# A two-block transformer forward pass in split precision: operand placement, attention bias tables, running sums, and GpSimd's part of the weight splits

## The reference

```
# first block
h = rmsnorm(x, norm_mix)
proj = h @ w_in           # z, xbc, dt | b q,k,v | c q,k,v, f | d q,kv | 4 gates of 1024
y_a = mamba2(...)         # causal conv, silu, y = (cb * exp(cum_l - cum_s)) @ (x dt), rmsnorm (ssm_norm_w)
y_b = softmax(q k / 8 + bias(distance), causal) @ v                 # "MoBA", one block of 256 here
y_c = softmax(q k / 8 + cum_f[q] - cum_f[k], causal) @ v            # "forgetting attention"
y_d = softmax(q k / 8 + bias(distance), window 128, with sinks) @ v # sliding window, 2 kv heads
x = x + (sum_i sigmoid(gate_i) * (y_i @ w_branch_i)) @ w_out
x = x + (silu(h2 @ w_gate) * (h2 @ w_up)) @ w_down                  # h2 = rmsnorm(x), inner width 2816
x = rmsnorm(x, norm_final)
# second block: two layers
x = x + hgrn2(rmsnorm(x)) ; x = x + swiglu(rmsnorm(x))
x = x + rglru(rmsnorm(x)) ; x = x + swiglu(rmsnorm(x)) ; out = rmsnorm(x)
```

## Time and profile before

| | us |
|---|---|
| three runs | 1255.49, 1258.89, 1253.69 (median 1255.49) |
| profiled execution | 1250.67 |
| its span | 1249.4 |

### The profile page before, as it was taken

How to read it: one execution, slowest core, us unless ns; L and a number is a source line. 1 busy time by engine, 2 the same in 40 slices (tenths; PEclk the granted TensorE clock), 3 DMA queues, 4 the chain that set the end, 5 groups by cost and what they waited for, 6 DMA issues and landing times.

```text
span 1249.4 us, 19584 instructions
## 1 busy us (share of the span) xinstructions
PE 1194.6 (96%) x8237; PEld 1096.5 (88%) x8237; DVE 682.3 (55%) x965; ACT 591.9 (47%) x901; POOL 473.1 (38%) x253
## 2 busy tenths in 40 slices
PE   7979999999989999999899999999999769999998
PEld 6979898788878999988898879999889768999986
DVE  5742644366756645334789757433326696633423
ACT  6534544445444554444652345444334674544432
POOL 4345333233231444441654423444423350543440
PEclk9989999999989999999999999999999879999999
DMA  7585465344445666564543435755555333756560
GB/s 240 163 265 154 145 197 144 108 121 125 128 135 152 184 188 187 187 200 143 182 134 135 151 120 171 217 177 185 196 185 173 114 135 118 217 181 187 177 199 34
DMA packets 160833, 204.75 MB, mean 164 GB/s; under 512 B 13535, under 2 KB 135577, under 8 KB 160746
## 3 DMA queue, kind: packets, MB, share of 16 engines
q1 hardware_dynamic: 154650, 193.69, 49.9%
q0 software_dynamic: 1840, 6.64, 1.6%
q10 hardware_dynamic: 4256, 3.16, 0.8%
HBM read 202.38 MB, written 1.09 MB: 163 GB/s over the span
## 4 chain that ended last, share of the span: by engine, by line
PE 78%; DVE 12%; ACT 6%; issue 2%; SPq 1%; ACTq 1%; DMA 0%; POOL 0%; DVEq 0%
PE bank L488 15%; PE bank L491 15%; PE bank L494 15%; PE bank L505 9%; PE bank L511 9%; PE bank L508 9%; ACT whi L947 2%; DVE wlo L1360 2%; DVE sm L1649 1%; PE bank L846 1%; DVE Ss L1780 1%; DVE ring L1651 1%; DVE uc L1490 1%; DVE qT L1774 1%; DVE ring L1637 1%
## 5 line engine op out<-in xcount | busy, mean ns | idle before, releaser
L1920 POOL TENSOR_TENSOR wlo<-raw,whi 128x1024 fp32r<-128x1024 f32 (+1 forms) x161 | 411.6, 2559 | 545.4 <-ACT whi L947 545.4
L947 ACT ACTIVATE whi<-raw 128x1024 fp32r<-128x1024 f32 x368 | 364.9, 1041 | 125.7 <-PE bank L511 117.0
L1360 DVE TENSOR_TENSOR wlo<-raw,whi 128x1024 fp32r<-128x1024 f32 x207 | 277.9, 1352 | 258.9 <-ACT whi L947 257.9
L488 PE MATMUL bank<-hh,whi 128*128 128x256 f32 x1792 | 293.7, 286 | 1.7 <-ACT hh L979 1.7
L491 PE MATMUL bank<-hh,wlo 128*128 128x256 f32 x1792 | 289.4, 284 | 0.9 <-DVE wlo L1360 0.9
L494 PE MATMUL bank<-hl,whi 128*128 128x256 f32 x1792 | 289.0, 284 | 0.0
L488 PEld LDWEIGHTS bank<-hh,whi 128*128 128x128 f32 x1792 | 248.8, 193 | 11.1 <-issue 9.9
L491 PEld LDWEIGHTS bank<-hh,wlo 128*128 128x128 f32 x1792 | 248.3, 193 | 1.4 <-DVE wlo L1360 1.4
L494 PEld LDWEIGHTS bank<-hl,whi 128*128 128x128 f32 x1792 | 248.4, 193 | 0.0
L505 PE MATMUL bank<-whi,gh 128*128 128x512 f32 x264 | 83.4, 397 | 0.0
L511 PE MATMUL bank<-whi,gl 128*128 128x512 f32 x264 | 83.1, 395 | 0.0
(11 more groups left out here) (296 smaller groups left out, 1319.0 us busy)
## 6 DMA issues: line engine op xcount, KB each, us to landing
raw<-in_ffn_w_in SPq DMA_DIRECT2D x88, 512.0 KB, 3.6
raw<-in_w_in SPq DMA_DIRECT2D x72, 512.0 KB, 3.7
raw<-in_ffn_w_out SPq DMA_DIRECT2D x44, 512.0 KB, 3.2
raw<-in_hgrn_w_in SPq DMA_DIRECT2D x32, 512.0 KB, 4.0
raw<-in_w_ffn_gate SPq DMA_DIRECT2D x22, 512.0 KB, 4.6
raw<-in_w_ffn_up SPq DMA_DIRECT2D x22, 512.0 KB, 4.1
raw<-in_w_ffn_down SPq DMA_DIRECT2D x22, 512.0 KB, 3.3
raw<-in_w_branch SPq DMA_DIRECT2D x16, 512.0 KB, 4.1
```

The lines of the kernel that those rows point to most:

```text
L488: T.matmul(out, wh[:, i, c], xh[:, k, :], start=first and (i, k) == pairs[0], stop=False)
L947: A.activation(half_of(whi, j, h), half_of(raw, j, h), ACT.Copy).then_inc(s_hi[j % NS][h], 1)
L1360: V.tensor_tensor(half_of(wlo, j, h), half_of(raw, j, h), half_of(whi, j, h).bitcast(f32), ALU.subtract).then_inc(s_lo[j % NS][h], 1)
L1920: G.tensor_tensor(half_of(wlo, j, 1), half_of(raw, j, 1), half_of(whi, j, 1).bitcast(f32), ALU.subtract).then_inc(s_lo[j % NS][1], 1)
```

## The change

It has six parts.

1. 64 bytes (`gap_hh`) are put in front of hh and hl. The antidiagonal matrix is no longer there, 288 bytes (`gap_stage`) are put behind the shared buffers, 64 bytes (`gap_bh`) behind `gate`, and `prow` is moved to the end. From the start of whi, modulo 512 bytes, hh goes from 0 to 64, bh from 320 to 64, gh from 160 to 0, and ch from 256 to 96.
2. The bias tables are read in falling order at once. For this GpSimd first copies the 16 rows 128 times within memory (`u_copies`, 3.1 MB), and the window's reading step for each partition becomes 383 numbers instead of 1. The flip products and their evacuations go.
3. Store and spreads of the running sums are issued by GpSimd.
4. ym is transposed into banks 3 and 7.
5. GpSimd makes wlo only for units 2 to 30 of each of the three feed-forwards, 87 halves. Before, it had 161 splits in all. VectorE makes the others.
6. The fills of the first attention are set out anew (b's four units over three steps, no window products).

The diff, cut to its core:

```diff
@@ buffers
         hn = sbuf(root, "hn", [128, 2, D])
+        sbuf(root, "gap_hh", [128, 16])
         hh = sbuf(root, "hh", [128, 8, 256], f32r)
...
-        flip = sbuf(root, "flip", [128, 128])
...
         half = sbuf(root, "half", [128, 16])
+        sbuf(root, "gap_stage", [128, 72])
...
-        prow = sbuf(mix, "prow", [128, 40])
         gate = sbuf(mix, "gate", [128, 2, 8, 256])
+        sbuf(mix, "gap_bh", [128, 16])
...
+        prow = sbuf(mix, "prow", [128, 40])
@@ who splits
-        starts = [unit_at[k] for k in (("g", 0, 0), ("hf", 0), ("g", 1, 0), ("lu", 0), ("g", 2, 0))] + [NU]
+        light = [(unit_at["g", f, 0] + 2, unit_at["g", f, 0] + 31) for f in range(3)]
         def on_pool(j, h):
-            return h == 1 and (j < 2 or j > 2) and all(not u - 2 <= j < u + 2 for u in starts)
+            return h == 1 and any(u0 <= j < u1 for u0, u1 in light)
@@ fills
-        FOX = [[("gate", 1, 0)], [("gate", 1, 1), ("ym",)], [("gate", 1, 2)], [("gate", 1, 3)], [("b", 0), ("b", 1)], [("b", 2)],
-               [("b", 3), ("bv",)], [("br", 0, 0)], [("br", 0, 1), ("win", 0)], [("win", 1), ("win", 2)]]
-        FOX_REST = [("win", c) for c in range(3, 8)]
+        FOX = [[("gate", 1, 0)], [("gate", 1, 1), ("ym",)], [("gate", 1, 2)], [("gate", 1, 3)], [("b", 0)], [("b", 1)],
+               [("b", 2), ("b", 3)], [("bv",)], [("br", 0, 0)], [("br", 0, 1)]]
@@ TensorE
-                        b = turn(("ym", c), 4 + c)
+                        b = turn(("ym", c), (3, 7)[c])
...
-                    T.matmul(banks[b][:, :], flip[:, :], windows_of(c), start=True, stop=True).then_inc(s_full[b], 1)
@@ ScalarE
                     A.activation(sums[:, :], banks[4][0:16, 0:256], ACT.Copy).then_inc(evacuated("sums"), 1)
-                    aq.wait_ge(*evac("sums"))
-                    A.dma_start(a["sums_scratch"], sums[:, :]).then_inc(s_sums, 16)
-            aq.wait_ge(s_sums, 16)
-            for rows, h0, parts in ((dec_rows, 0, ((0, 0, 256), (256, 128, 128))), (fox_rows, 8, ((0, 0, 128), (128, 0, 256)))):
...
-                        A.dma_start(rows[i][:, :, c0:c0 + n], src).then_inc(s_spread[h0 // 8], 16)
...
-                    A.activation(windows_of(what[1]), bank_of(*what)[:, :], ACT.Copy).then_inc(evacuated(*what), 1)
@@ VectorE, the logits of an attention
                     if n == 1:
                         vq.wait_ge(s_masked, 2)
+                    else:
+                        vq.wait_ge(s_w, 32)
@@ GpSimd
             G.dma_start(a["u_scratch"], rb[0:16, 16:400]).then_inc(s_u, 16)
-            use(("cv", 1), 0)
+            gq.wait_ge(*evac("sums"))
+            G.dma_start(a["sums_scratch"], sums[:, :]).then_inc(s_sums, 16)
+            gq.wait_ge(s_sums, 16)
+            for rows, h0, parts in ((dec_rows, 0, ((0, 0, 256), (256, 128, 128))), (fox_rows, 8, ((0, 0, 128), (128, 0, 256)))):
...
+                        G.dma_start(rows[i][:, :, c0:c0 + n], src).then_inc(s_spread[h0 // 8], 16)
...
-                    use(("gate", 0, 1))
+                    gq.wait_ge(s_u, 16)
+                    G.dma_start(a["u_copies"], a["u_scratch"].rearrange("h (o n) -> h o n", o=1).broadcast_to([16, 128, 384])).then_inc(s_copies, 16)
...
-                    gq.wait_ge(s_u, 16)
+                    gq.wait_ge(s_copies, 16)
...
-                        src = bass.AP(a["u_scratch"].tensor, 8 * i * 384, [[1, 128], [384, 8], [1, 256]])
+                        src = bass.AP(a["u_copies"].tensor, 8 * i * 128 * 384 + 127, [[383, 128], [128 * 384, 8], [1, 256]])
```

More of the change, by code:

```diff
@@ L397, in hn_set @@
             return s_hn, HN[e] + i + 1
-        CONST = {k: i + 1 for i, k in enumerate(["ident", "ones", "flip", "half", "pad", "tri"])}
+        CONST = {k: i + 1 for i, k in enumerate(["ident", "ones", "half", "pad", "tri"])}
         def const(name):
             return s_const, CONST[name]
-        FOX = [[("gate", 1, 0)], [("gate", 1, 1), ("ym",)], [("gate", 1, 2)], [("gate", 1, 3)], [("b", 0), ("b", 1)], [("b", 2)],
-               [("b", 3), ("bv",)], [("br", 0, 0)], [("br", 0, 1), ("win", 0)], [("win", 1), ("win", 2)]]
-        FOX_REST = [("win", c) for c in range(3, 8)]
+        FOX = [[("gate", 1, 0)], [("gate", 1, 1), ("ym",)], [("gate", 1, 2)], [("gate", 1, 3)], [("b", 0)], [("b", 1)],
+               [("b", 2), ("b", 3)], [("bv",)], [("br", 0, 0)], [("br", 0, 1)]]
         MOBA = [[("d", 0)], [("d", 1)], [("dk",)], [("dv",)], [("br", 1, 0)], [("br", 1, 1)], [("gate", 2, 0)], [("gate", 2, 1)], [], []]
@@ L754, in fill, with attention @@
                         tok.then_inc(s_full[b], 1)
[L755 to L760, removed]
-                    T.matmul(banks[b][:, :], flip[:, :], windows_of(c), start=True, stop=True).then_inc(s_full[b], 1)
-            def attention(n, fills, rest, inputs):
+            def attention(n, fills, inputs):
                 q, k, v, heads_k, window, slot = ATT[n]
@@ L803, in attention @@
                         values(i - 2)
[L804 to L810, removed]
+            attention(1, FOX, [("col", "c", j) for j in range(4)] + [("tok", "cv", t) for t in range(2)])
+            attention(2, MOBA, [("col", "b", j) for j in range(4)] + [("tok", "bv", t) for t in range(2)])
+            attention(3, SWA, [("col", "d", 0), ("col", "d", 1), ("col", "dk"), ("dv",)])
             branch(3, 0)
@@ L1124, in fill, with attention @@
                         A.activation(bh[:, 0, 2 * c:2 * c + 2, :], two(bank_of("ym", c)[:, :]), ACT.Copy).then_inc(s_bt, 1)
-                else:
-                    aq.wait_ge(*full(*what))
-                    A.activation(windows_of(what[1]), bank_of(*what)[:, :], ACT.Copy).then_inc(evacuated(*what), 1)
-            def attention(n, fills, rest):
+            def attention(n, fills):
                 slot = ATT[n][5]
@@ L1171, in attention @@
                         values_out(i - 2)
[L1172 to L1177, removed]
+            attention(1, FOX)
+            attention(2, MOBA)
+            attention(3, SWA)
             branch(3, 0)
@@ L1620, in fill, with attention @@
                                         ALU.subtract).then_inc(evacuated("ym", c), 1)
-                elif what[0] != "win":
+                else:
                     use(what)
-            def attention(n, fills, rest):
+            def attention(n, fills):
                 window, slot = ATT[n][4:]
@@ L1943, in gpsimd_program @@
             G.memset(vec[0:1, :], 1.0).then_inc(s_const, 1)
-            diagonal(flip, -127, 1).then_inc(s_const, 1)
             G.memset(half[:, :], -0.5).then_inc(s_const, 1)
@@ L1959, in gpsimd_program @@
             G.dma_start(a["u_scratch"], rb[0:16, 16:400]).then_inc(s_u, 16)
-            use(("cv", 1), 0)
+            gq.wait_ge(*evac("sums"))
+            G.dma_start(a["sums_scratch"], sums[:, :]).then_inc(s_sums, 16)
+            gq.wait_ge(s_sums, 16)
+            for rows, h0, parts in ((dec_rows, 0, ((0, 0, 256), (256, 128, 128))), (fox_rows, 8, ((0, 0, 128), (128, 0, 256)))):
+                for c0, s0, n in parts:
+                    for i, heads in enumerate((5, 3)):
+                        src = bass.AP(a["sums_scratch"].tensor, (h0 + 5 * i) * 256 + s0, [[0, 128], [256, heads], [1, n]])
+                        G.dma_start(rows[i][:, :, c0:c0 + n], src).then_inc(s_spread[h0 // 8], 16)
             for i, (rows, step) in enumerate(((dec_rows, 1), (fox_rows, -1))):
@@ L1987, in fill @@
                     for i, dst in enumerate((wmoba, wswa)):
-                        src = bass.AP(a["u_scratch"].tensor, 8 * i * 384, [[1, 128], [384, 8], [1, 256]])
+                        src = bass.AP(a["u_copies"].tensor, 8 * i * 128 * 384 + 127, [[383, 128], [128 * 384, 8], [1, 256]])
                         G.dma_start(dst, src).then_inc(s_w, 16)
-                elif what[0] != "win":
+                else:
                     use(what)
-            for fills in (*FOX, FOX_REST, *MOBA, *SWA):
+            for fills in (*FOX, *MOBA, *SWA):
                 for what in fills:
```

9 lines of the change are left out of this document (3 added, 6 removed).

## The result

The changed kernel takes 1213.5 us (median of 4 runs, 1206.7 to 1216.0) against 1254.6 of the kernel before (4 runs, 1252.4 to 1258.9). The ratio is 0.966, with an interval of 0.961 to 0.971. Forecast were 1212 and, from the rows, -42.7 us; the medians differ by 41.1, and the two profiled executions by 39.0 (1211.7 against 1250.7).

The account below looks back on a forecast made before the run. TensorE's matmul streaming, plus a few waits with low clock behind them, was taken as the bound. Terms sum to -42.7 us from 1250.7, giving 1208.0; adding the median's 4.8, rounded down, gives 1212, range 1186 to 1232.

Parts of the forecast that it names:

- Moving operand: 5376 matmuls with hh or hl moving, now 64 bytes off, speed up to 117.5 to 117.6 ns: -11.8 us.
- Rival A: Matmuls on the normed input settle at bh's short spacing, 113 ns: 24 us more gain, 1188 us; chance 0.20.
- Rival B: Placement does nothing, the rates belong to other things than the offset: +17.5 us, 1230 us; chance 0.13.
- Rival E: Offset 64 slows the moving operand like gh's case, 7.2 ns on each of 5376 matmuls: 1267 us; chance 0.05.
- item 2: Feed-forward inner parts: 792 matmuls with gh or gl stationary gain -5.7 us; 528 with hh stationary taken as 0.
- Sums: First transposes: spreads off ScalarE's queue remove TensorE's 6.5 us wait and low clock behind it: -8.8 us.
- Rival C: GpSimd's queue delivers the sums late, masks at 102, TensorE stands before the first mamba product: +9, 1221 us; chance 0.13.
- ym: Third scores: new banks remove TensorE's 3.0 us wait and half of 6.8 us at clock 0.50: -6.4 us.
- Bias tables: First attention: flip products and last table's wait go, the 3.1 MB copy is hidden: -7.8 us.
- The term for the third attention's tail: Wait before L782: a VectorE split of 1.22 us and a free L1649 give -1.2 us with what follows.
- LRU's -1.0: LRU stage: L1860 gets shorter, one split is added on that chain: -1.0 of the 9.6 us wait.
- item 6: 74 splits move to VectorE, +90 us work, nearly offset by unblocked instructions; path gains -1.2 and -1.0 us, HGRN 0.

Follow-up runs that it names:

- e1: The kernel before with only the new placement of buffers; ratio to before 0.991, 1240.7 against 1250.8 us.
- e2: The changed kernel with hh and hl back at offset 0 from the weights; ratio to the kernel before 0.975, 1219.8 us.
- e8: The changed kernel with every buffer moved by 64 bytes, all relations kept; the text given shows no time for it.
- e11: The changed kernel with hh and hl 320 bytes from the weights instead of 64; 320 ran as 64, no time in the text given.
- e10: The changed kernel with hh and hl 192 bytes from the weights instead of 64; 113.1 ns per matmul in one stretch, no total time in the text given.
- e3: The changed kernel with store and eight spreads of the running sums issued by ScalarE again; ratio to the kernel before 0.976.
- e5: The changed kernel with ym transposed into banks 4 and 5 again; a TensorE wait of 2.7 us returned and 4.3 us were lost there.
- e6: The kernel before with only the bias tables read in falling order from copies, without flip products, and the new fills; ratio 0.994, 1243.2 against 1252.2 us.
- e4: The kernel before with only the new rule for which engine makes wlo; ratio 0.996, 1246.1 against 1250.8 us.

## Why the prediction was right, point by point

1. Moving operand: right in value (117.6 taken, 117.6 measured) and in the reason, the relation to the weights modulo 256, which e1, e2, e8 and e11 show. Rival A's 113 ns exists, but at 64 in only 5 of 113 groups; it is the rule at 192 (e10). Rival B falls with e1. Rival E, offset 64 bad for the moving operand, is wrong for it and true for the stationary one.
2. gh: right (-5.7 forecast, -5.1 measured). The prediction writes that gh at 160 is 96 modulo 256; it is 160, and no row had a stationary operand at 96. The number of item 2 doesn't rest on that. The 528 matmuls with stationary hh were taken at 0 between -3.8 and +3.8 and cost +2.9: the row at 160 was slow and that at 0 fast, so a loss at 64 was likelier than a gain. Items 1 and 2 together were forecast at -17.5; the spacings give -14.6, and e1 alone gained only 10.2 us (8.5 to 13.9 by its interval). Placement was thus worth less than the sum had it.
The rule of the Trainium skill's page "SBUF — State Buffer" (Who interferes with whom), that TensorE has two independent read ports and waits on nobody, would have made e1 a null as the prediction read it. The measured 835 and 851 per 100 us do not fit that reading.
3. Sums: right (-8.8 forecast; -9.4 at the jump in the trace, 8.3 lost in e3). GpSimd's and ScalarE's rows around the place in the changed kernel:

```profile
81.88 3.36 POOL L1942 DMA_DIRECT2D decs<-sums_scratch  x4 [2.24 <-DMA sums_scratch<-sums]
...
93.47 4.37 POOL L1949 TENSOR_SCALAR_AFFINE_SELECT decs<-decs 128x640 f32<-128x640 f32 x4 [4.89 <-DMA decs<-sums_scratch]
```
```profile
84.82 1.08 ACT L1050 ACTIVATE area<-bank 128x512 f32<-128x512 f32 x2
...
98.38 0.60 ACT L957 ACTIVATE qkv<-bank 128x512 f32<-128x512 f32 x1 [2.20 <-PE bank L510]
98.87 0.50 ACT L1066 ACTIVATE decs<-decs,am 128x256 f32<-128x256 f32 x1
```
The masks are done at 97.84, later than the 96 taken, and ScalarE's exponentials start at 98.87, right behind the evacuation that its order puts first: 1.0 us of slack. Rival C did not happen, but was near. The eight issues took 6.7 us, 0.84 each, no longer than the 0.92 of the earlier trace rows; so the starvation of GpSimd's DMAs that the "DVE blocks DMA" trap of the Trainium skill's page "SBUF — State Buffer" describes did not show in the issues. The landings were later than from ScalarE's queue, before and after; why was not tested:

```profile
decs<-sums_scratch ACTq DMA_DIRECT2D x1, 640.0 KB, 5.7
...
decs<-sums_scratch POOLq DMA_DIRECT2D x1, 640.0 KB, 7.3
```
4. ym: the mechanism is right, and the trace agrees (-6.4 forecast, -6.3 measured), but partly by luck. The kernel before was profiled in an execution with 6.8 us at 0.50 behind the wait, where four other traces have 3.4 us; against those the banks are worth 4.3 (e5).
5. Bias tables: right (-7.8 forecast; -7.8 in e6). The copy landed 18.1 us after issue, twice the 9.5 us reckoned at full rate, and still early: it was issued at 97.8, and the loads from it at 144.8. Nothing waited for weights beyond 0.8 us on ScalarE (1.8 before). The copy's row:

```profile
u_copies<-u_scratch POOLq DMA_DIRECT2D x1, 3072.0 KB, 18.1
```
6. Splits: the balance on VectorE was right (its busy time went from 682 to 672 us though 74 splits came to it), and so was the 22 us that L1651's operation alone gives back (29.0 to 6.9 in e4). The term for the third attention's tail was mis-sized: -1.2 forecast, -5.5 measured (e4). The step that failed is "now a split of 1.22 and a free L1649: -1.2 with what follows". It counted what one step saves. In e4 the splits and the quotient take 2.42 us against 3.44, so about 1.0 is saved, as reckoned; but the last three steps of this attention all had the long quotient (2.36, 2.35 and 2.30 us), and in e4 VectorE comes to the last step with time in hand: one step earlier it idles 1.53 us for TensorE's scores, where before it didn't. So TensorE's whole wait of 3.0 us went. And the low clock behind the wait was not reckoned, though items 3 and 4 had reckoned theirs. LRU's -1.0 is not shown: the wait went from 9.6 to 9.2 us in the changed kernel and to 10.9 in e4, so the stage's gain of about 1 us in both isn't the shorter chain that the prediction had in mind.

What the sum missed: 2.9 us lost before 70 us. That and the smaller gain of placement offset the larger gain of item 6, which is why the total came out so close; the closeness of 1212 to 1213.5 is in part luck.

## What to carry to other kernels

When one form of matmul streams at two speeds in a trace, compare the placement of its operands relative to each other before anything else; a sweep over offsets at 32 or 64 bytes costs one run each and gave here more than any of the reordered instructions. Try each offset for the moving and the stationary role apart, since what helps one can harm the other. When a wait is removed, reckon the low clock behind it with it, but as a range: behind waits of 2.5 to 3.2 us at one place it was 3.4 us in four traces and 6.8 in one.

## What the runs showed of the hardware that was not expected

- The mean spacing of 128x256 matmuls depends on the moving operand's offset from the stationary one, and 320 is as 64: 119.9 ns at 0, 116.8 at 32, 117.6 at 64, 118.8 at 128, 114.2 at 192 (113.1 in the long stretch). With the roles changed, 512 columns: 227 to 228 at 0, 232 to 235 from 32 to 160, 229.6 at 192. Why 192 is not the mirror of 64 is open. So is why ch, at 96, had 119.9, and what chooses between 113 and 118 ns from one group to the next at one offset.
- The granted clock fell without a wait ahead of it, here behind narrow matmuls. In the changed kernel TensorE was busy without a gap from 34 us on, but from 39.23 on with matmuls of 16 columns (dtf), and the clock was at 0.50 from 41.7 to 51.9:

```profile
39.23 0.95 PE L504 MATMUL bank<-whi,hh 128*128 128x16 f32 x8
```
```profile
42.00:52.00 10.00, 10.00 (x37) 8.94 (x38) 8.15 (x14) 5.43 (x7) 0.00 (x0) 0.50 0.57 167
```
The kernel before ran the same narrow matmuls and had 0.50 from 45.3 to 48.7 only. Between the 0th and the 96th hl matmul the kernels with the new splitting rule lost from 2.1 to 7.2 us against the kernel before (eleven traces, with 6.8 to 17.0 us at 0.50 before 70 us, where it had 3.4). The two without the rule, e1 and e6, lost 2.5 and 1.4, with 10.2 and 6.8 us. The rule alone (e4) lost 6.4, with 17.0 us. So the rule may have a part in it, but it is one trace of each kernel, and the two groups overlap; it isn't shown. The scatter of the changed kernel's four runs goes with the clock: 1206.7 us at a mean of 0.988, 1216.0 at 0.981.
